# Attention in a hybrid diffusion step: a sixth PSUM bank, the waits of a pair of scores taken together, and the value products moved ahead of the next turns

## The chip, the cores and the metric

The kernel runs on one core of a Trainium2 chip. The metric is the device time in microseconds (us) of one execution. The kernel before takes 1153.21 us, the median of 3 runs (1152.54 to 1154.63).

The engines are named as in the profile: PE is TensorE (its matmuls; PEld is its weight loads), DVE is VectorE, ACT is ScalarE, POOL is GpSimd, SP is SyncE. Each engine works through its own program in order and stops at a wait until another engine has raised a semaphore. PSUM, where PE puts its results, has 8 banks of 512 float32 numbers for each of the 128 partitions.

## The reference: what is computed

Two trunk layers on 384 tokens (128 context tokens and 256 latent tokens) of width 1024, in float32. The even layer runs a Mamba-2 scan and latent attention (MLA, 8 heads) side by side, the odd layer grouped-query attention (GQA, 16 query heads of width 64); each ends with a mixture of 16 experts. What the change touches is the attention of both layers:

```
def block_attention(q, k, v):            # queries in blocks of 128
    ...
        s = jnp.einsum('bqgrd,bkgd->bgrqk', qi, k, preferred_element_type=jnp.float32) * scale
        p = jax.nn.softmax(s, axis=-1).astype(v.dtype)
        return jnp.einsum('bgrqk,bkgv->bqgrv', p, v)
```

The context tokens see 128 keys. The latent tokens see 384 keys: 128 of a cache and their own 256. With three blocks of 128 queries a head has three such tiles, so there are 24 tiles in MLA and 48 in GQA.

## The kernel before, in words

The program is written by hand, engine by engine, and the order in the text is the order in which an engine works. In the attention, the unit u is one tile of 128 queries of one head. `unit(u)` (L226) gives the head and the block: heads go in pairs, and the six units of a pair are block 0 of both heads (128 keys), block 1 of both, block 2 of both (384 keys each).

A unit goes through these steps:

- PE, L482: the scores, 128 queries by 128 or 384 keys, into a PSUM bank. In MLA the operands have 96 rows, in GQA 64; the two heads of a GQA pair stand in different halves of the 128 rows.
- DVE, L1293: minus the maximum of each row.
- ACT, L910: the exponential, from the bank into one of four buffers in `Pb` (unit u uses buffer u modulo 4), and the row sums. Ahead of it ACT waits for three things: the scores, the maximum, and the turn of unit u-4, which must have left the same buffer: `if u >= 4: after((kind, "pT", u - 4))`, in `exponential`.
- DVE, L1298 and L1300: one over the row sum, and the scaling.
- PE, L489: the turn, that is one or three 128x128 transposes, into another bank.
- ACT, L925: the turned rows are copied out of the bank into a turned-row buffer. There are two buffers, one for each head of a pair, so the copy of block 0 of a later pair first waits until the value products of the pair before are done (`pv_done`).
- PE, L504 and L507, in `values`: when all six units of a pair are turned and copied (`pt_ready`), the products of the values and the turned rows, for both heads, into bank 5 or 6.
- DVE, L1310, in `pair_out`: the result out of the bank.

PE and ACT go through the units in steps of two. In the step that begins at unit `first`, PE puts the scores of units first and first+1, then the turns of units first-4 and first-3 (`AHEAD` is 4), and then, in every third step, the value products of the pair whose last turns were in the step before. ACT puts the exponentials of units first and first+1, then the copies of units first-4 and first-3. So in the step with the value products of one pair, the scores and exponentials are those of block 2 of the next pair, and the turns and copies those of block 0 of that next pair.

The banks: every result that PE leaves in PSUM for ACT or DVE is a "job", listed once for the whole program (`job`, `attention_jobs`), with the engine that empties it. Job j goes into bank j modulo 5 (`RB` is 5), and `fill` makes PE wait until job j-5 has been emptied. The value products have banks 5 and 6 for themselves, bank 7 holds the rows of the modulation (`modulation`, L1219 to L1228, reads them; the call with part 2 stands behind the MLA attention in DVE's program).

Of the kernel before, what the change touches and what calls it, by code (L numbers as in the profile page):

```python
# [26 lines left out]
NT = T // P  # L27
# [47 lines left out]
def build(nc, small_d, x_d, w_d, y_d, stf_d, stb_d, ckv_d, kpe_d, gk_d, gv_d):  # L75
# [7 lines left out]
    with ctx:  # L83
# [67 lines left out]

        m_att = region(3072 + CONV_C * 385 + 3072 + 1536, 4 * 384, 2 * 896, 24, 24)
        lsq, lr_both = hTt[:, 0:1152], hTt[:, 1152:1920]
        lr = [lr_both[:, 0:384], lr_both[:, 384:768]]
# [6 lines left out]
        gss = [gss[:, HQ * t:HQ * (t + 1)] for t in range(NT)] + [gss[:, NT * HQ + HKV * t:NT * HQ + HKV * (t + 1)] for t in range(NT)]  # L161
        g_att = [gP, gPT, gnm, grs]
        qkv3 = qkv.rearrange("p (t n) -> p t n", t=NT)
        gkT3 = gkT.rearrange("p (h n) -> p h n", h=HKV)
        gqT3 = hTt[:, :].rearrange("p (h n) -> p h n", h=8)
# [47 lines left out]
        jobs = []  # L213
# [95 lines left out]
        free_of = {"A": S["free_act"], "D": S["free_dve"]}  # L309
        bank = lambda j: ps[:, j % RB, :]  # L310

# [79 lines left out]
        def _(pe):  # L391
            at = [0]

            def fill(*name):

                j = at[0]
                assert jobs[j][0] == name, (jobs[j], name)
                if j >= RB:
                    by, n = emptied[j - RB]
                    pe.wait_ge(free_of[by], n)  # L400
                at[0] += 1
                return bank(j)
# [68 lines left out]
            def attention(kind, heads, q_of, k_of, v_of, places):  # L471

                Pb, PTb = places[:2]
                base = 0 if kind == "mla" else NT * HM
                pairs = 0 if kind == "mla" else HM // 2
                for first in range(0, NT * heads + AHEAD, 2):
                    for u in (first, first + 1):
                        if u < NT * heads:
                            h, t = unit(u)
                            k0, nk = KEYS[t]  # L480
                            b = fill(kind, "s", u)
                            filled(mm(b[:, 0:nk], q_of(t, h), k_of(h, k0, nk), start=True, stop=True))  # L482
                    for v in (first - AHEAD, first - AHEAD + 1):
                        if v >= 0:
                            h, t = unit(v)
                            pe.wait_ge(S["p_ready"], base + v + 1)
                            b = fill(kind, "pT", v)
                            for k in range(KEYS[t][1] // P):
                                ins = pe.transpose(b[:, P * k:P * k + P], Pb[:, 384 * (v % 4) + P * k:384 * (v % 4) + P * k + P], ident)  # L489
                            filled(ins)  # L490
                    done = first - AHEAD
                    if done > 0 and done % 6 == 0:
                        values(done // 6 - 1, base, pairs, v_of, PTb)
                values(heads // 2 - 1, base, pairs, v_of, PTb)

            def values(k, base, pairs, v_of, PTb):
                pe.wait_ge(S["pt_ready"], base + 2 * NT * (k + 1))
# [3 lines left out]
                rows = [slice(0, 64), slice(64, 128)]  # L501
                pt = [PTb[:, 896 * i:896 * i + 896] for i in range(2)]
                for i in range(2):
# [272 lines left out]
            for k in range(N_PREP + 1):  # L776
# [11 lines left out]
                if k:  # L788
                    pe.wait_ge(S["qk_ready"], k)
                    for hh in range(2):  # L790
# [3 lines left out]
                        filled(ins)  # L794
            pe.wait_ge(S["qkT_ready"], 2 * N_PREP)
            attention("mla", HM, lambda t, h: mqT3[0:QM, h, TILE[t]], lambda h, k0, nk: mkT3[0:QM, h, k0:k0 + nk],
                      lambda s, h: mv3[:, s, 64 * h:64 * h + 64], m_att)
# [43 lines left out]
        def _(act):  # L841
# [56 lines left out]
            def attention(kind, heads, places):  # L898
                Pb, PTb, nm, rs = places
                base = 0 if kind == "mla" else NT * HM  # L900
# [14 lines left out]
                def turned(v):  # L915
                    h, t = unit(v)
                    b = take(kind, "pT", v)
                    if t == 0 and h >= 2:
                        act.wait_ge(S["pv_done"], base // NT + h // 2 * 2)
                    pt = PTb[:, 896 * (h % 2):896 * (h % 2) + 896]  # L920
                    out, src = pt[:, 0:P], b[:, 0:P]
# [264 lines left out]
        def _(dve):  # L1186
# [96 lines left out]
            def attention(kind, heads, places, out):  # L1283
                Pb, PTb, nm, rs = places
                base = 0 if kind == "mla" else NT * HM
# [303 lines left out]
            for k in range(N_PREP + 1):  # L1589
# [10 lines left out]
                if k:  # L1600
                    v = k - 1
                    s = v - NT
                    t = v if s < 0 else s
                    on = t in (1, 2)
                    qk_norm(v, cut(mkt[v % 2], HM), HM, QM, sm("q_norm" if s < 0 else "k_norm"), mss[v % 2], cut(msq[v % 2], HM),
                            rot("cos_e", t, ROPE) if on else None, rot("sin_e", t, ROPE) if on else None, NOPE)
                    dve.sem_inc(S["qk_ready"], 1)
            attention("mla", HM, m_att, oTm3)
            modulation(2)
            residual(0, 2, "out")  # L1610
# [204 lines left out]
```

## Time and profile before

| | |
|---|---|
| median of 3 runs | 1153.21 us (1152.54 to 1154.63) |
| the profiled execution's own time | 1165.88 us |
| its span in the trace | 1163.0 us |
| mean granted clock of TensorE | 0.892 of full speed |
| MLA attention, first scores to the output projection | 403.2 to 440.8 us of the span |
| GQA attention, first scores to the output projection | 821.2 to 897.2 us of the span |
| PE, DVE, ACT busy over the span | 80%, 32%, 26% |

The profiled execution is one run, 12.67 us above the median of the runs without a profile. All durations and positions below are of that execution. A view of the order of work gives for each group of instructions its start and duration and, in brackets, how long its engine stood idle before it and what the idle time ended with. "ACTq" as a releaser is ACT's sequencer, which raises a semaphore by an instruction of its own, as in the hand-back of a PSUM bank at L913 and L927. "issue" is a wait for nothing that the profile shows. "PEclk" is the mean granted clock of TensorE in the stretch, as a share of full speed (2.4 GHz); its lower level is 0.5 (1.2 GHz).

### The profile page before, as it was taken

To read this page: it belongs to the slowest core of one execution; us is meant where nothing else is said; L and a number is where in the kernel's file an instruction comes from. 1 tells how busy PE (TensorE), PEld (TensorE's weight loads), DVE (VectorE), ACT (ScalarE), POOL (GpSimd) and SP (SyncE) were. 2 spreads that over 40 slices of the span, in tenths; PEclk is the share of its full clock that TensorE was granted. 3 is DMA by queue.
4 is the path that set the end of the run, shared out by engine and by line. 5 is a ranking of instruction groups with operands and counts; after the bars stand their busy time and mean duration, and the time that the engine had idled before them with its cause. 6 is when DMAs were issued, how large, how long until landed. Compare 5 with 4: busy or idle time off the path is not lost.

```text
span 1163.0 us, 13763 instructions
## 1 busy us (share of the span) xinstructions
PE 934.8 (80%) x5481; PEld 488.7 (42%) x5481; DVE 375.5 (32%) x918; ACT 297.4 (26%) x690; POOL 50.3 (4%) x63
## 2 busy tenths in 40 slices
PE   5999985777886689972999991799898972999992
PEld 1455643555643445532323321455444532323321
DVE  0322015655734470042111101444664142101113
ACT  1421031232424370040201111311665140101111
POOL 0300000000000000102000001000000102000001
PEclk8899998978978799985999995799789985999995
DMA  9999994542464401215599997004100125599934
GB/s 387 427 424 413 413 420 203 214 163 109 158 239 162 168 1 55 109 55 198 226 408 424 424 425 283 0 1 179 47 1 1 58 105 205 234 412 414 418 144 181
DMA packets 36193, 258.96 MB, mean 223 GB/s; under 512 B 3392, under 2 KB 3536, under 8 KB 21152
## 3 DMA queue, kind: packets, MB, share of 16 engines
q1 hardware_dynamic: 20304, 198.27, 42.5%
q0 software_dynamic: 12224, 47.01, 10.2%
q10 hardware_dynamic: 3600, 12.78, 2.7%
q8 instruction: 45, 0.74, 0.3%
q14 instruction: 20, 0.16, 0.0%
HBM read 203.17 MB, written 54.87 MB: 222 GB/s over the span
## 4 chain that ended last, share of the span: by engine, by line
PE 66%; DVE 14%; DMA 8%; ACT 6%; issue 3%; POOL 1%; another core or an unknown queue 1%; POOLq 0%; SPq 0%; DVEq 0%; ACTq 0%
PE ps L468 20%; PE ps L580 12%; PE ps L602 7%; PE ps L817 6%; DMA U<-expert_rows 3%; DMA expert_rows<-U 3%; PE ps L482 3%; PE ps L564 2%; PE ps L432 2%; DMA ring<-w_in 2%; PE ps L507 2%; PE ps L736 2%; PE ps L489 1%; PE ps L528 1%; DVE U L1535 1%
## 5 line engine op out<-in xcount | busy, mean ns | idle before, releaser
L580 PE MATMUL ps<-ring,U 128*32 128x512 f32 x1200 | 166.3, 592 | 0.0
L468 PE MATMUL ps<-U,ring 128*128 128x384 f32 x320 | 105.1, 487 | 2.7 <-DVE U L1310 1.4
L602 PE MATMUL ps<-ring,U 128*32 128x512 f32 x672 | 85.7, 594 | 0.0
L580 PEld LDWEIGHTS ps<-ring,U 128*32 128x32 f32 x1200 | 47.5, 110 | 85.4 <-issue 85.4
L468 PEld LDWEIGHTS ps<-U,ring 128*128 128x128 f32 x320 | 60.0, 189 | 47.4 <-issue 4.2
L580 PE MATMUL ps<-hT,U 128*32 128x512 f32 x168 | 73.1, 592 | 0.0
L580 PE MATMUL ps<-U 128*32 128x512 f32 x168 | 73.1, 592 | 0.0
L817 PE MATMUL ps<-ring,hT 128*128 128x384 f32 x192 | 65.9, 503 | 5.8 <-ACT hT L895 4.9
L432 PE MATMUL ps<-ring,cond_w 128*32 128x384 f32 x512 | 58.3, 581 | 14.5 <-ACT cond_w L872 8.6
L468 PE MATMUL ps<-hT,ring 128*128 128x384 f32 x208 | 68.6, 488 | 1.0 <-issue 1.0
L564 PE MATMUL ps<-small,U 128*128 128x128 f32 x192 | 31.8, 318 | 44.7 <-DMA U<-expert_rows 42.5
L1393 DVE TENSOR_TENSOR U<-ps,U 128x256 f32<-128x256 f32 x24 | 10.1, 422 | 135.0 <-ACT U L963 135.0
L468 PEld LDWEIGHTS ps<-hT,ring 128*128 128x128 f32 x208 | 39.0, 190 | 30.0 <-issue 4.0
L817 PEld LDWEIGHTS ps<-ring,hT 128*128 128x128 f32 x192 | 37.3, 197 | 33.3 <-issue 9.6
L482 PE MATMUL ps<-U,hT 64*128 64x128 f32 (+3 forms) x144 | 48.6, 513 | 3.2 <-ACTq L913 1.6
L564 PEld LDWEIGHTS ps<-small,U 128*128 128x128 f32 x192 | 24.6, 162 | 54.5 <-DMA U<-expert_rows 48.5
L1401 DVE COPY U<-ps 128x512 f32<-128x512 f32 x24 | 16.6, 692 | 93.9 <-PE ps L602 53.6
L651 PE MATMUL ps<-small,U 128*128 128x128 f32 x48 | 11.8, 426 | 43.4 <-DVE U L1431 43.4
L884 ACT ACTIVATE hT<-xT 128x384 f32<-128x384 f32 x32 | 15.2, 516 | 110.1 <-DVE xT L1252 105.6
L963 ACT ACTIVATE U<-ps 128x256 f32<-128x256 f32 x24 | 9.3, 386 | 131.7 <-PE ps L580 131.7
L1252 DVE SCALAR_TENSOR_TENSOR xT<-ps,misc,xT 128x128 f32<-128x128 f32 (+1 forms) x32 | 11.9, 412 | 96.0 <-PE ps L468 96.0
L468 PE MATMUL ps<-ring,hT 128*128 128x384 f32 (+1 forms) x144 | 42.0, 451 | 0.5 <-issue 0.5
(251 smaller groups left out, 1337.8 us busy)
## 6 DMA issues: line engine op xcount, KB each, us to landing
ring<-w_in SPq DMA_DIRECT2D x102, 1536.0 KB, 11.2
expert_rows<-U POOLq DMA_DIRECT2D x16, 2048.0 KB, 73.1
U<-expert_rows SPq DMA_DIRECT2D x24, 512.0 KB, 6.0
expert_rows<-U ACTq DMA_DIRECT2D x24, 512.0 KB, 9.5
hT<-w_in SPq DMA_DIRECT2D x6, 1536.0 KB, 12.6
U<-w_in SPq DMA_DIRECT2D x6, 1536.0 KB, 15.8
small<-small_in SPq DMA_DIRECT2D x1, 3147.5 KB, 34.3
xT<-x_in SPq DMA_DIRECT2D x1, 1536.0 KB, 16.7
```

The source lines that it names most:

```text
L432: ins = mm(ps[q:q + 32, bank_row, 0:384], cond3[:, k, :], w[:, k, :], start=(k < 4), stop=(k >= 4))
L468: ins = mm(out, lhs(k), rhs(k), start=(k == 0), stop=(k == n - 1))
L482: filled(mm(b[:, 0:nk], q_of(t, h), k_of(h, k0, nk), start=True, stop=True))
L507: ins = mm(ps[rows[i], 5 + pair % 2, P:T], v_of(1 + c, 2 * k + i), pt[i][:, P + 256 * c:P + 256 * c + 256], start=(c == 0), stop=(c == NT ...
L564: ins = pe.transpose(ps[:, 3 + h, P * c:P * c + P], xgb[i % NR][:, 512 * h + P * c:512 * h + P * c + P], ident)
L580: ins = mm(ps[q:q + 32, r, :], xgT[:, r, P * k + q:P * k + q + 32], w[e][:, c:c + 512], start=(k == 0), stop=(k == DC - 1))
L602: ins = mm(ps[q:q + 32, 6 + h, :], actT_of[i % NR][:, P * j + q:P * j + q + 32], w[e][:, c:c + 512], start=(j == 0), stop=(j == 1))
L736: ins = mm(ps[:, 5 + q // 2, 64 * hh:64 * hh + 64], dec[u % 3][:, P * h:P * h + P], xdt[d][:, 64 * (4 * q + h):64 * (4 * q + h) + 64], sta ...
L817: ins = mm(b[:, 0:384], hT[:, k, TILE[t]], w[:, k, :], start=(k == 0), stop=(k == DC - 1))
L884: A(hT[:, c, :], xT[:, c, :], ACT.Square).then_inc(S["sq_ready"], 1)
L1252: ins = stt(xT[:, c, SEG[s]], b[:, SEG[s]], gt[:, 2 * c + s:2 * c + s + 1], xT[:, c, SEG[s]], MUL, ADD)
L1401: dve.tensor_copy(ysb[i % 2][:, 512:1024], ps[:, 7, :]).then_inc(S["y_dve"], 1)
```

## The change

In the attention of both layers:

- Bank 7 joins the five banks of the jobs while attention jobs are filled. Which bank a job gets is now worked out in a list, the bank longest unused first, and `fill` waits for the job that last had that bank. With six banks the pattern of four jobs to a step (two scores, two turns) gives the scores the banks of the turns two steps back, and the turns the banks of the scores one step back.
- PE waits for the banks of both scores of a pair before it puts the first, so the two score products stand next to each other without a wait between them.
- The value products of a step stand behind its scores and ahead of its turns; before, they stood behind its turns.
- GQA has four buffers of turned rows instead of two (two of them in the rows of queries that are no longer needed), and the copy of block 0 waits for the value products of two pairs back. MLA keeps its two buffers.
- Bank 7 must be free for the MLA attention: DVE's `modulation(2)`, which reads it, stands ahead of the attention, and PE waits for it (`mod_ready`).

The exponential's wait for the turn of unit u-4, the number of `Pb` buffers, and all instructions with their shapes stay as they are.

```diff
+        m_att[1] = [m_att[1][:, 896 * i:896 * i + 896] for i in range(2)]
...
-        g_att = [gP, gPT, gnm, grs]
+        g_att = [gP, [gPT[:, 0:896], gPT[:, 896:1792], qkv3[:, 1, 0:896], qkv3[:, 2, 0:896]], gnm, grs]
...
-        bank = lambda j: ps[:, j % RB, :]
+        order, last, BANK, BEFORE = deque(range(RB)), {}, [], []
+        for j, (n, _) in enumerate(jobs):
+            if n[0] in ("mla", "gqa"):
+                if RB + 2 not in order:
+                    order.appendleft(RB + 2)
+            elif RB + 2 in order:
+                order.remove(RB + 2)
+            b = order.popleft()
+            order.append(b)
+            BANK.append(b)
+            BEFORE.append(last.get(b))
+            last[b] = j
+        bank = lambda j: ps[:, BANK[j], :]
...
-                if j >= RB:
-                    by, n = emptied[j - RB]
+                if BEFORE[j] is not None:
+                    by, n = emptied[BEFORE[j]]
                     pe.wait_ge(free_of[by], n)
...
                 for first in range(0, NT * heads + AHEAD, 2):
-                    for u in (first, first + 1):
-                        if u < NT * heads:
+                    if first < NT * heads:
+                        b2 = [fill(kind, "s", u) for u in (first, first + 1)]
+                        for u in (first, first + 1):
                             h, t = unit(u)
                             k0, nk = KEYS[t]
-                            b = fill(kind, "s", u)
-                            filled(mm(b[:, 0:nk], q_of(t, h), k_of(h, k0, nk), start=True, stop=True))
+                            filled(mm(b2[u - first][:, 0:nk], q_of(t, h), k_of(h, k0, nk), start=True, stop=True))
+                    done = first - AHEAD
+                    if done > 0 and done % 6 == 0:
+                        values(done // 6 - 1, base, pairs, v_of, PT)
                     for v in (first - AHEAD, first - AHEAD + 1):
...
-                    done = first - AHEAD
-                    if done > 0 and done % 6 == 0:
-                        values(done // 6 - 1, base, pairs, v_of, PTb)
...
-                    if t == 0 and h >= 2:
-                        act.wait_ge(S["pv_done"], base // NT + h // 2 * 2)
-                    pt = PTb[:, 896 * (h % 2):896 * (h % 2) + 896]
+                    if t == 0 and h >= len(PT):
+                        act.wait_ge(S["pv_done"], base // NT + h // 2 * 2 - len(PT) + 2)
+                    pt = PT[h % len(PT)]
...
             pe.wait_ge(S["qkT_ready"], 2 * N_PREP)
+            pe.wait_ge(S["mod_ready"], len(PARTS))
             attention("mla", HM, lambda t, h: mqT3[0:QM, h, TILE[t]], lambda h, k0, nk: mkT3[0:QM, h, k0:k0 + nk],
...
+            modulation(2)
             attention("mla", HM, m_att, oTm3)
-            modulation(2)
```

PE's program in the GQA attention, in the step that holds the value products of the first pair, with the semaphores that each row waits for; `ps` is PSUM, `U` the work area, `hT` holds the queries and `small` the identity. The rows of before are the scores of block 2 (L482), the turns of block 0 (L489), the value products (L504, L507) and the scores of the next step:

```order
L482 MATMUL ps<-U,hT 128x384 [waits free_act] x2
L489 MATMUL ps<-small,U 128x128 [waits free_act,p_ready] x2
L504 MATMUL ps<-U 64x128 [waits pt_ready]
L504 MATMUL ps<-U 64x128
L507 MATMUL ps<-U,small 64x256 x2
L507 MATMUL ps<-U 64x256 x4
L482 MATMUL ps<-U,hT 128x128 [waits free_act] x2
```

The same place in the changed program, where L495 are the scores, L505 the turns, L517 and L520 the value products:

```order
L495 MATMUL ps<-U,hT 128x384 [waits free_act]
L495 MATMUL ps<-U,hT 128x384
L517 MATMUL ps<-U 64x128 [waits pt_ready]
L517 MATMUL ps<-U 64x128
L520 MATMUL ps<-U,small 64x256 x2
L520 MATMUL ps<-U 64x256 x4
L505 MATMUL ps<-small,U 128x128 [waits free_act,p_ready] x2
L495 MATMUL ps<-U,hT 128x128 [waits free_act]
L495 MATMUL ps<-U,hT 128x128
```

The two turns have moved behind the value products, with their wait for `pt_ready` ahead of them, and the second score of each pair has lost its wait for a bank.

DVE's program at the beginning of the MLA attention, before (L1279 ends the preparation of the keys, L1293 are the first maxima):

```order
L1278 TENSOR_TENSOR U<-U 128x768
L1279 TENSOR_TENSOR U<-U,small 128x768
L1293 TENSOR_REDUCE U<-ps 128x1 x2
L1298 RECIPROCAL U<-U 128x1
L1300 TENSOR_SCALAR U<-U 128x128
```

and now, where L1240 is the modulation's one instruction:

```order
L1292 TENSOR_TENSOR U<-U 128x768
L1293 TENSOR_TENSOR U<-U,small 128x768
L1240 TENSOR_TENSOR misc<-ps,small 128x96
L1307 TENSOR_REDUCE U<-ps 128x1 x2
L1312 RECIPROCAL U<-U 128x1
```

The modulation stands ahead of the first maxima; before, it stood behind the last copy of the attention.

## Rows read from the trace of the kernel before

**Rows 1.** The page's busy times over the span, three engines of its section 1.
```profile
PE 934.8 (80%) x5481; PEld 488.7 (42%) x5481; DVE 375.5 (32%) x918; ACT 297.4 (26%) x690; POOL 50.3 (4%) x63
```

**Rows 2.** Busy time by stretch: two GQA turns and one of MLA.
```profile
core 0: us, PE busy (x) PEld busy (x) DVE busy (x) ACT busy (x) POOL busy (x), PEclk, DMA share, GB/s
863.74:871.91 8.17, 7.64 (x43) 4.00 (x43) 5.86 (x19) 6.06 (x18) 0.00 (x0) 1.00 0.01 2
...
425.07:433.26 8.19, 7.58 (x42) 4.21 (x42) 5.77 (x19) 6.06 (x18) 0.00 (x0) 1.00 0.00 1
```

**Rows 3.** Order of work on ACT, one GQA turn at full clock.
```profile
866.56 0.37 ACT L910 ACTIVATE U<-ps,U 128x128 f32<-128x128 f32 x1 [0.21 <-PE ps L489]
...
867.81 1.08 ACT L925 COPY U<-ps 128x384 f32<-128x384 f32 x2
869.10 0.58 ACT L910 ACTIVATE U<-ps,U 128x384 f32<-128x384 f32 x1 [0.21 <-PE ps L489]
...
870.77 1.08 ACT L925 COPY U<-ps 128x384 f32<-128x384 f32 x2
872.07 0.58 ACT L910 ACTIVATE U<-ps,U 128x384 f32<-128x384 f32 x1 [0.21 <-DVE U L1293]
872.95 0.58 ACT L910 ACTIVATE U<-ps,U 128x384 f32<-128x384 f32 x1 [0.21 <-ACT U L910]
873.80 0.27 ACT L925 COPY U<-ps 128x128 f32<-128x128 f32 x1 [0.18 <-PE ps L507]
```

**Rows 4.** Order of work on PE and DVE in the same turn.
```profile
870.84 0.30 PE L489 MATMUL ps<-small,U 128*128 128x128 f32 x1
...
871.44 0.30 PE L489 MATMUL ps<-small,U 128*128 128x128 f32 x1 [0.30 <-DVE U L1300]
...
871.91 0.44 PE L504 MATMUL ps<-U 128*64 128x128 f32 x4 [0.17 <-ACT U L925]
...
872.61 1.03 PE L507 MATMUL ps<-U 128*64 128x256 f32 x8
...
873.57 0.49 PE L482 MATMUL ps<-U,hT 64*128 64x128 f32 x4
873.72 0.56 DVE L1310 COPY U<-ps 128x384 f32<-128x384 f32 x1 [0.33 <-PE ps L507]
```

**Rows 5.** Waits in the GQA attention, then in the MLA attention.
```profile
PEld ps L482 <- ACTq L913: 6.5, 13, 0.9
...
PEld ps L482 <- ACTq L927: 1.4, 6, 0.2
...
PEld ps L482 <- ACTq L913: 4.0, 8, 0.7
...
PEld ps L482 <- ACTq L927: 0.7, 3, 0.2
```

**Rows 6.** Order of work on PE, then on ACT: value products at the lower clock.
```profile
844.06 0.69 PE L504 MATMUL ps<-U 128*64 128x128 f32 x4 [0.16 <-ACT U L925]
...
847.24 0.51 PE L482 MATMUL ps<-U,hT 64*128 64x128 f32 x4
```
```profile
847.45 0.27 ACT L925 COPY U<-ps 128x128 f32<-128x128 f32 x1 [1.68 <-PE ps L507]
...
857.29 0.27 ACT L925 COPY U<-ps 128x128 f32<-128x128 f32 x1 [1.57 <-PE ps L507]
...
891.63 0.27 ACT L925 COPY U<-ps 128x128 f32<-128x128 f32 x1 [1.67 <-PE ps L507]
```

**Rows 7.** Busy time and granted clock by stretch, MLA and GQA.
```profile
407.00:440.80 33.80, 28.23 (x161) 15.68 (x159) 21.74 (x71) 23.33 (x68) 0.00 (x0) 1.00 0.01 1
821.20:833.70 12.50, 11.66 (x35) 6.48 (x36) 7.48 (x26) 7.92 (x23) 0.00 (x0) 0.50 0.03 10
...
843.90:847.30 3.40, 3.24 (x18) 1.72 (x18) 0.71 (x3) 1.45 (x5) 0.00 (x0) 0.50 0.02 5
```

**Rows 8.** Order of work on ACT at the beginning of the GQA attention.
```profile
829.92 0.37 ACT L910 ACTIVATE U<-ps,U 128x128 f32<-128x128 f32 x1 [0.41 <-PE ps L489]
...
833.08 0.58 ACT L910 ACTIVATE U<-ps,U 128x384 f32<-128x384 f32 x1 [0.82 <-PE ps L489]
```

**Rows 9.** Order of work on DVE around the MLA attention.
```profile
403.80 0.56 DVE L1293 TENSOR_REDUCE U<-ps 128x1 f32<-128x128 f32 x2 [5.01 <-PE ps L482]
...
440.63 0.25 DVE L1226 TENSOR_TENSOR misc<-ps,small 128x96 f32<-128x96 f32 x1
```

More of the change, by code:

```diff
@@ L471, in attention @@
             def attention(kind, heads, q_of, k_of, v_of, places):
-                Pb, PTb = places[:2]
+                Pb, PT = places[:2]
                 base = 0 if kind == "mla" else NT * HM
@@ L490, in attention, with values @@
                             filled(ins)
-                    done = first - AHEAD
-                    if done > 0 and done % 6 == 0:
-                        values(done // 6 - 1, base, pairs, v_of, PTb)
-                values(heads // 2 - 1, base, pairs, v_of, PTb)
-            def values(k, base, pairs, v_of, PTb):
+                values(heads // 2 - 1, base, pairs, v_of, PT)
+            def values(k, base, pairs, v_of, PT):
                 pe.wait_ge(S["pt_ready"], base + 2 * NT * (k + 1))
@@ L501, in values @@
                 rows = [slice(0, 64), slice(64, 128)]
-                pt = [PTb[:, 896 * i:896 * i + 896] for i in range(2)]
+                pt = [PT[(2 * k + i) % len(PT)] for i in range(2)]
                 for i in range(2):
@@ L898, in attention @@
             def attention(kind, heads, places):
-                Pb, PTb, nm, rs = places
+                Pb, PT, nm, rs = places
                 base = 0 if kind == "mla" else NT * HM
@@ L1283, in attention @@
             def attention(kind, heads, places, out):
-                Pb, PTb, nm, rs = places
+                Pb, _, nm, rs = places
                 base = 0 if kind == "mla" else NT * HM
```

## The prediction

> **What bounds the kernel now.** I read the page first, then the order of work inside the two attentions, since the change touches nothing else. Over the span PE is busiest and ACT is at 26% [rows 1], which says nothing about this stage. A stretch from one start of the value products to the next is the time of one pair of heads (a turn of the loop, three steps): 8.17 us in GQA, 8.19 in MLA, at full clock in both [rows 2]. The two agree, though the scores of MLA have 96 rows and cannot stand beside each other in the array as those of GQA might; PE is busy 7.6 of the 8.2 us and ACT 6.06, so by busy time PE looks like the bound [rows 2].
>
 The reader is to see in rows 3 that the exponential at 872.07 starts 0.22 us behind the copies that end at 871.85 (870.77 + 1.08), and in rows 4 that PE begins the value products at 871.91, released by the same copies. The two run beside each other. They can, because the two turns of block 0, which this exponential and its neighbour wait for, stand on PE ahead of the values, at 870.84 and 871.44 [rows 4].
>
> PE's waits are real as waits: its score loads waited 6.5 + 1.4 us in GQA and 4.0 + 0.7 in MLA for ACT to hand back a bank [rows 5]. But they end when ACT, the slower of the two, gets there.
>
> **The change, part by part.** Sums are made against the profiled execution (span 1163.0 us, own time 1165.88); the median of the runs is 12.67 us less. I carry the difference over to the median unscaled.
>
> Values ahead of turns. In the step with value products, ACT's exponential of unit u (block 2) waits for the turn of unit u-4, which is the turn of block 0 of the next pair. In the changed order this turn stands behind the value products on PE. The value products in turn wait for `pt_ready`, that is for the two copies which ACT makes directly ahead of that exponential. So ACT, which had the values beside its exponentials, now has them in its chain: copies, values, turn, exponential. Step by step, from 871.85, where the copies end:
> - to the start of the values 0.06 us (871.91) [rows 4];
> - the values until PE takes its next instruction, 873.57 - 871.91 = 1.66 us [rows 4];
> - one transpose, 0.30 us [rows 4];
> - from PE's end to the next engine, 0.08 us (the last value product ends at 872.61 + 1.03 = 873.64, DVE's copy starts at 873.72) [rows 4].
>
> That puts the exponential at 873.95 instead of 872.07, 1.88 us later. The second exponential needs the second transpose, which is ready long before its turn 0.88 us later. Queued behind ACT's waiting exponential are the second exponential and the copies of block 0; everything on ACT moves by 1.88 us, and nothing gives it back, as ACT has no idle time in the rest of the turn. The next turn takes about 8.17 + 1.88 = 10.05 us. Value products stand inside the loop 3 times in MLA (4 pairs, the last behind the loop) and 7 times in GQA (8 pairs): 10 x 1.88 = +18.8 us. The shortest the rows allow is the 1.66 and the 0.06 alone, less the 0.21 that ACT needs anyhow: 1.51 us, 15.1 in all. The longest is values to their last end (1.73), 0.06, 0.30, and a hand-over to ACT of 0.21 as before its exponentials: 2.30 - 0.21 = 2.09, 20.9 in all. I take 1.88, which is the sum of the neighbours' own rows.
>
> At the lower clock the values take 847.24 - 844.06 = 3.18 us instead of 1.66, and before, ACT already stood idle 1.68, 1.57 and 1.67 us for them at three of the seven GQA pairs [rows 6]. There the new chain is longer by 1.52 and the old wait of about 1.5 (less the 0.18) goes away, so these three add the same 1.9 us each.
>
> Sixth bank and the joint wait. They take away PE's waits for ACT's hand-backs [rows 5] and let the two GQA scores of a pair run side by side. At full clock this is beside ACT's chain and worth nothing. Its cover is gone where PE is the slower one: the beginning of GQA, at half clock up to 833.7 us [rows 7], where ACT waited 0.41 and 0.82 us for PE, 0.81 us more than its 0.21 each time [rows 8]. I take -0.8 us; the bounds are 0 and, for all four bank waits of rows 5, -12.6, which is a rival below. The joint wait itself can hold a first score back for the second's bank; both are banks of turns two steps back, which ACT emptied a step before, so I put it at nothing.
>
> Four turned-row buffers. They free the copy of block 0 from the pair before; but that copy now stands behind a turn that stands behind the same values. At full clock it waited for nothing (0.18 us is the fixed cost). Nothing.
>
> Modulation and its wait. It takes 0.25 us behind the attention [rows 9]. DVE is idle 5.01 us ahead of the first maximum of MLA [rows 9], which hides it, and PE's wait for it stands where PE waits for ACT's last copies anyhow. Without this cover it would cost 0.25 us.
>
> The clock. PE gets longer pauses for the same work: a turn of 10.05 us holds what 8.17 held. In GQA PE fell to the lower clock for three short stretches inside the loop, each time at value products [rows 6, 7]; in MLA from 407 us on it never did [rows 7]. Each new such stretch that holds value products costs 3.18 - 1.66 = 1.52 us on the chain. I take one to two more, +2.3 us; the bounds are 0 and 7 x 1.52 = 10.6.
>
> Sum: 18.8 - 0.8 + 2.3 = +20.3 us, so 1153.2 + 20.3 = 1173.5 us. In the profiled execution I expect MLA some 6 us longer and GQA some 14.
>
> **Rivals.**
>
> Banks were the bound (faster). PE waits at L482 for ACT's hand-back in nearly every step, and by busy time PE is the fullest engine. If PE's waits set the pace, taking them away gives back up to 6.5 + 1.4 + 4.0 + 0.7 = 12.6 us [rows 5]: 1140.6 us. It decides if ACT has slack of more than 1.9 us in a turn, so that the late exponential is absorbed. For it: PE's 7.6 us of 8.17 [rows 2]. Against it: the constant gaps of ACT [rows 3], and that MLA and GQA turns last the same. The Trainium skill, on its page "Perfetto Trace Analysis", section "Optimization Strategy", says that the same gap repeating on the engine that should be saturated can mean too few buffers in SBUF or PSUM. By that rule the sum would be this rival's 1140.6. The trace shows the repeating gap on PE, but not that PE is the engine to be saturated here.
>
> The values are early enough (no change). If the value products could start before ACT's copies end, only the transpose behind them would be late, 873.57 + 0.30 + 0.08 = 873.95 against the copy at 873.80: 0.15 us for each of the ten, 1154.7 us. It would need the exponential not to wait for that turn, or `pt_ready` to be asked for an earlier unit. The program has both waits unchanged, and rows 4 show the values starting 0.06 us behind the copies. Only a slip in my reading speaks for it.
>
> The clock falls with the pauses (slower still). If PE loses full clock at all seven of the ten value products that had it, the sum is 18.8 - 0.8 + 10.6 = +28.6 us, 1181.8 us. For it: three falls in GQA already, with pauses of 0.3 us. Against it: MLA has none in 33.8 us [rows 7], and the value products themselves are dense work. The Trainium skill describes it on the page "TensorE: Matmul & The Clock Gate", section "A second HAM failure mode: psum-queue depth-cycling": short idle times of PE between groups, as PSUM banks are cycled, make the clock swing between its two levels. By that the sum would be this rival's 1181.8; the trace agrees for GQA in three places and disagrees for MLA.
>
> **How the numbers follow.** My forecast has 0.80, the clock rival 0.14, no change 0.03, the banks 0.03. What can be told from no change is about 0.2%, 2.3 us. The forecast's own bounds are 15.1 - 0.8 = +14.3 and 20.9 - 0.8 + 4.6 (three slow stretches) = +24.7, so 1167.5 to 1177.9. To hold the time 8 times in 10 I let the range reach to the clock rival: 1167 to 1182. Slower by over 0.2%: 0.94; within: 0.03; faster: 0.03.
>
> **What would show it.** Right: in a turn, ACT has one idle time of about 2 us, ahead of the block 2 exponential, put down to PE's turn, and it follows the copies and covers the value products; the other gaps stay at 0.21 and 0.12 to 0.18. A turn lasts about 10 us. The waits of the scores for ACT's bank hand-back shrink and the GQA scores of a pair overlap, with no gain. DVE is idle 2 to 3 us once in a turn. Nothing outside the two attentions changes length. Wrong: turns of 8.2 us or less with a 0.21 gap there, or turns of 10 us in one attention only, or a change of time in the scan or the experts.

## The result, and the profile after

The changed kernel takes 1177.11 us, the median of 4 runs (1171.84 to 1187.82). The kernel before, run on the same chip beside it, takes 1153.15 us (1152.54 to 1154.63, 4 runs). The ratio is 1.0192, with a 95% interval of 1.0137 to 1.0247: slower by 1.4 to 2.5%. The forecast was 1173.5 us, in a range of 1167 to 1182. Here and below, ratios and intervals are computed from the single runs, without those in a slower state, so they are not exactly the quotients of the medians.

The profiled execution took 1187.82 us, with a span of 1185.9 us, the longest of the four. It stands 10.71 us above its median, much as that of before does (12.67). Its stages, and the same of the profile before, in us:

| stage | before | after | difference |
|---|---|---|---|
| start to the first MLA scores | 403.17 | 406.07 | +2.90 |
| MLA attention | 37.60 | 45.28 | +7.68 |
| output projection | 64.10 | 66.65 | +2.55 |
| experts, and the projections of the odd layer | 316.29 | 315.28 | -1.01 |
| GQA attention | 76.06 | 85.87 | +9.81 |
| output projection | 42.80 | 45.27 | +2.47 |
| last experts | 222.95 | 221.44 | -1.51 |

The attentions and the projections behind them are 22.5 us longer together, of the 22.9 us between the two spans. The ratio gives 0.0192 x 1153.15 = 22.1 us, so these four stages hold the loss.

Busy time and granted clock by stretch, of the kernel after (columns as in [rows 2]). The first row is a turn of the loop in MLA, the second one in GQA. The other three are the beginning of MLA, and the last value products of each attention with the start of the output projection:

```profile
430.40:440.44 10.04, 7.31 (x42) 4.38 (x42) 5.70 (x20) 6.07 (x18) 0.00 (x0) 1.00 0.00 1
857.13:867.16 10.03, 6.31 (x43) 3.39 (x43) 5.71 (x20) 6.05 (x18) 0.00 (x0) 1.00 0.00 1
...
406.10:412.20 6.10, 6.10 (x13) 3.58 (x14) 3.45 (x13) 3.54 (x9) 0.00 (x0) 0.50 0.10 40
446.30:456.50 10.20, 8.40 (x24) 4.53 (x25) 0.56 (x1) 0.95 (x2) 0.00 (x0) 0.50 0.00 0
917.40:924.20 6.80, 6.12 (x14) 3.10 (x11) 0.56 (x1) 0.00 (x0) 0.00 (x0) 0.50 0.00 0
```

A turn has gone from 8.17 and 8.19 us [rows 2] to 10.03 and 10.04. All engines do the work they did: ACT 6.05 us against 6.06, DVE 5.71 against 5.86. PE in GQA is even less busy, 6.31 us against 7.64. A longer turn with no more work is a longer chain. The order of work on ACT shows where it is:

```profile
856.01 1.07 ACT L939 COPY U<-ps 128x384 f32<-128x384 f32 x2
859.25 0.58 ACT L924 ACTIVATE U<-ps,U 128x384 f32<-128x384 f32 x1 [2.17 <-PE ps L505]
...
860.12 0.58 ACT L924 ACTIVATE U<-ps,U 128x384 f32<-128x384 f32 x1 [0.20 <-ACT U L924]
...
860.97 0.27 ACT L939 COPY U<-ps 128x128 f32<-128x128 f32 x1 [0.17 <-ACT U L924]
...
862.53 0.37 ACT L924 ACTIVATE U<-ps,U 128x128 f32<-128x128 f32 x1 [0.20 <-ACT U L924]
```

One gap of 2.17 us stands where [rows 3] have 0.21, and it is put down to a turn, L505. The others are what they were. The order of work on PE in the same turn shows what this turn stands behind:

```profile
857.13 0.44 PE L517 MATMUL ps<-U 128*64 128x128 f32 x4 [1.88 <-ACT U L939]
857.40 0.60 PE L520 MATMUL ps<-U,small 128*64 128x256 f32 x4
...
857.84 1.03 PE L520 MATMUL ps<-U 128*64 128x256 f32 x8
...
858.80 0.44 PE L505 MATMUL ps<-small,U 128*128 128x128 f32 x2
859.17 0.49 PE L495 MATMUL ps<-U,hT 64*128 64x128 f32 x4
...
864.36 0.92 PE L495 MATMUL ps<-U,hT 64*128 64x384 f32 x4 [0.67 <-ACTq L941]
```

ACT's copies end at 857.08 (856.01 + 1.07). The values start at 857.13, the turn behind them at 858.80, ACT's exponential at 859.25. Each step of the chain is there. PE now stands idle 1.88 us ahead of the values (in [rows 4]: 0.17), and ACT 2.17 us behind them: the two engines wait for each other in turn. The last row is a pair of GQA scores without a wait between them: their four records span 0.92 us, and PE is idle 0.67 us ahead of them for a bank.

DVE (the first row is the modulation, in its new place):

```profile
403.31 0.26 DVE L1240 TENSOR_TENSOR misc<-ps,small 128x96 f32<-128x96 f32 x1 [2.79 <-PEq L451]
...
407.02 0.61 DVE L1307 TENSOR_REDUCE U<-ps 128x1 f32<-128x128 f32 x2 [3.44 <-PE ps L495]
```

The waits of the kernel after, in GQA and then in MLA (columns as in [rows 5]: us in total, times, longest):

```profile
PEld ps L517 <- ACT U L939: 18.5, 8, 2.5
ACT U L924 <- PE ps L505: 18.3, 12, 3.8
...
PEld ps L495 <- ACTq L941: 7.8, 12, 0.9
...
ACT U L924 <- PE ps L505: 7.4, 4, 2.2
...
PEld ps L495 <- ACTq L941: 3.2, 6, 0.6
```

A sixth bank did not remove PE's waits for banks in GQA: the score loads waited 7.8 us for L941 and once 1.2 us for L927, against 6.5 + 1.4 in [rows 5]. The waits have changed hands: L941 hands back a bank of copied turns, where L913 handed back a bank of scores. The turns now wait for L927, the hand-back of the scores: 4.5 us, against 0.6 us for turns before. So the change moved the waits of PE and did not take them away.

### The profile page after: what moved, and what is told of

Its sections match the earlier page's. It is cut to its first block, busy times and chain, and to the rows that moved or that the text cites. A ratio compares the mean times of both kernels' runs of the same rounds, so it can differ in the third digit from the quotient of the medians.

```text
span 1185.9 us, 13795 instructions
## 1 busy us (share of the span) xinstructions
PE 935.6 (79%) x5481; PEld 490.7 (41%) x5481; DVE 375.2 (32%) x918; ACT 297.6 (25%) x690; POOL 50.4 (4%) x63
## 4 chain that ended last, share of the span: by engine, by line
PE 64%; DVE 13%; DMA 8%; ACT 8%; issue 4%; POOL 1%; another core or an unknown queue 1%; ACTq 0%; POOLq 0%; SPq 0%; DVEq 0%
PE ps L481 19%; PE ps L593 12%; PE ps L615 7%; PE ps L831 6%; DMA U<-expert_rows 3%; DMA expert_rows<-U 3%; PE ps L577 2%; ACT U L924 2%; ACT U L939 2%; PE ps L495 2%; PE ps L445 2%; DMA ring<-w_in 2%; PE ps L749 2%; PE ps L520 2%; DVE U L1549 1%
## 5 line engine op out<-in xcount | busy, mean ns | idle before, releaser
L481 PE MATMUL ps<-U,ring 128*128 128x384 f32 x320 | 110.1, 505 | 2.7 <-DVE U L1324 1.4
L481 PEld LDWEIGHTS ps<-U,ring 128*128 128x128 f32 x320 | 62.5, 197 | 50.7 <-issue 8.9
L495 PE MATMUL ps<-U,hT 64*128 64x128 f32 (+3 forms) x144 | 39.3, 532 | 9.2 <-ACTq L941 6.9
L924 ACT ACTIVATE U<-ps,U 128x384 f32<-128x384 f32 (+1 forms) x72 | 36.8, 510 | 37.2 <-PE ps L505 25.7
L664 PE MATMUL ps<-small,U 128*128 128x128 f32 x48 | 11.8, 427 | 42.8 <-DVE U L1445 42.8
```

What stands on the lines that cost most here:

```text
L481: ins = mm(out, lhs(k), rhs(k), start=(k == 0), stop=(k == n - 1))
L495: filled(mm(b2[u - first][:, 0:nk], q_of(t, h), k_of(h, k0, nk), start=True, stop=True))
L924: A(Pb[:, 384 * (u % 4):384 * (u % 4) + nk], b[:, 0:nk], ACT.Exp, bias=nm[:, u:u + 1], accum_out=rs[:, u:u + 1]).then_inc(S["e_ready"], 1)
```

## The experiments

Two theories were put to the test. By the first, the new time is a chain: the value products stand between ACT's copies and the turn that ACT's next exponential waits for. By the rival, it comes from the banks: the joint wait, or the sixth bank's new pattern.

**Value products back behind the turns.** All else of the change stays.

```diff
-                    done = first - AHEAD
-                    if done > 0 and done % 6 == 0:
-                        values(done // 6 - 1, base, pairs, v_of, PT)
                     for v in (first - AHEAD, first - AHEAD + 1):
...
                             filled(ins)
+                    done = first - AHEAD
+                    if done > 0 and done % 6 == 0:
+                        values(done // 6 - 1, base, pairs, v_of, PT)
```

> The changed kernel with the value products put back behind the turns of the step; sixth bank, joint wait, four turned-row buffers and the moved modulation stay. Theory (the turn of block 0 behind the values puts the values into ACT's chain): turns of 8.2 us again, ACT's gap ahead of the block 2 exponential 0.21 us, time 1152 to 1154 us. Rival (the new bank order, the joint wait and a lower clock that follows from them are the cost): turns stay near 9 to 10 us or PE falls to the lower clock more often, time 1162 us or more. Second rival (PE's bank waits were the bound and are now gone): turns below 8 us, time 1141 to 1147 us.

Measured: 1157.75 us (1153.67 to 1166.92, 12 runs) beside 1153.66 of before (23 runs), ratio 1.0028, interval 0.9995 to 1.0061. The loss is gone, though the time is above the 1152 to 1154 us that I had expected. There is no gain either: the sixth bank, the joint wait and the four buffers together are worth nothing that can be measured. They were not put in one by one, but for the joint wait (below). The order of work on ACT, of this kernel, has the old short gaps behind the copies and ahead of block 0:

```profile
838.79 1.07 ACT L939 COPY U<-ps 128x384 f32<-128x384 f32 x2
840.06 0.58 ACT L924 ACTIVATE U<-ps,U 128x384 f32<-128x384 f32 x1 [0.20 <-DVE U L1307]
...
841.78 0.27 ACT L939 COPY U<-ps 128x128 f32<-128x128 f32 x1 [0.17 <-PE ps L520]
```

The turn that holds it, by stretch, shows PE busy for 1.5 us less than in [rows 2] and the turn only 0.1 us shorter:

```profile
838.79:846.83 8.04, 6.09 (x42) 3.48 (x42) 5.83 (x20) 6.06 (x18) 0.00 (x0) 1.00 0.01 3
```

**Only the value products moved.** The kernel before, with five banks and single waits, and the same three lines of `values` ahead of the turns.

```diff
+                    done = first - AHEAD
+                    if done > 0 and done % 6 == 0:
+                        values(done // 6 - 1, base, pairs, v_of, PTb)
                     for v in (first - AHEAD, first - AHEAD + 1):
...
-                    done = first - AHEAD
-                    if done > 0 and done % 6 == 0:
-                        values(done // 6 - 1, base, pairs, v_of, PTb)
```

> The kernel before with one edit, the value products ahead of the turns of the step; five banks, single waits, two turned-row buffers. Theory: the whole loss, turns of about 10.1 us in both attentions, one idle time of about 2.0 to 2.2 us on ACT ahead of the block 2 exponential, time 1170 to 1178 us. Rival (the loss needs the sixth bank and the joint wait): turns of at most 9 us, time below 1162 us.

Measured: 1181.15 us (1176.46 to 1182.57, 4 runs), ratio 1.0228, interval 1.0175 to 1.0282. One edit brings the whole loss; its interval overlaps that of the full change. The turns are 10.13 us at full clock, as expected, and the time is above the expected 1170 to 1178 us. On ACT the same gap:

```profile
426.52 1.08 ACT L925 COPY U<-ps 128x384 f32<-128x384 f32 x2
...
429.78 0.58 ACT L910 ACTIVATE U<-ps,U 128x384 f32<-128x384 f32 x1 [2.18 <-PE ps L492]
```

Its GQA attention is 92.44 us in the profile, 6.6 more than that of the full change, because the clock was low for longer there, as one stretch shows:

```profile
884.10:901.00 16.90, 16.32 (x55) 8.98 (x54) 8.21 (x26) 9.06 (x27) 0.00 (x0) 0.50 0.00 0
```

**Six exponential buffers.** The changed kernel, but the exponential of unit u waits for the turn of unit u-6, which is ahead of the values again. This leaves the values where the change put them and cuts the chain.

```diff
+        g_att = [[gP[:, 384 * i:384 * i + 384] for i in range(4)] + [gPT[:, 384 * i:384 * i + 384] for i in range(2)],
+                 [gPT[:, 896:1792]] + [qkv3[:, i, 0:896] for i in range(3)], gnm, grs]
...
-                    if u >= 4:
-                        after((kind, "pT", u - 4))
+                    if u >= 6:
+                        after((kind, "pT", u - 6))
```

> The changed kernel, values ahead of the turns as in it, with six buffers for the exponentials instead of four, so that the exponential of unit u waits for the turn of unit u-6 and not u-4. Theory: the exponentials of block 2 run beside the value products again and only the copy of block 0 is late, by about 0.15 us: turns of 8.3 to 8.4 us, time 1153 to 1157 us. Rival (what costs is the place of the values among PE's work, whatever the exponential waits for): turns stay at 10.0 us, time 1170 us or more.

Measured: 1160.61 us (1156.57 to 1169.62, 10 runs), ratio 1.0077, interval 1.0036 to 1.0118. Turns at full clock take 8.31 us in MLA and 8.33 to 8.34 in GQA, as expected; the time is above the expected 1153 to 1157 us. The order of work on ACT, then on PE:

```profile
829.90 0.65 ACT L941 COPY U<-ps 128x128 f32<-128x128 f32 x2 [0.33 <-PE ps L507]
...
835.07 1.08 ACT L941 COPY U<-ps 128x384 f32<-128x384 f32 x2
836.36 0.58 ACT L926 ACTIVATE U<-ps,U 128x384 f32<-128x384 f32 x1 [0.21 <-DVE U L1309]
```

```profile
836.21 0.44 PE L519 MATMUL ps<-U 128*64 128x128 f32 x4 [1.91 <-ACT U L941]
```

The exponential at 836.36 now runs beside the values, which begin at 836.21.

The gap of 2.17 us is gone with the values still ahead of the turns, so it is the wait for u-4 that makes them cost, and not their place as such. What stays is the turn itself: the copies of block 0 wait for it 0.33 us instead of 0.17. Ten times 0.14 us are 1.4 us of the 4 to 14 us that the interval gives; the rest is not shown. In its profile the two attentions are 3.0 us longer than before (38.30 and 78.36 us), and PE fell to the lower clock at five value products in GQA, against three before.

**Block 0 copied by DVE.** ACT's chain is 6.05 us of busy time and its fixed gaps. Here the value products are behind the turns and the copies of block 0 go from ACT to DVE, behind the scaling of the pair's last unit.

```diff
-                    job((kind, "pT", u - AHEAD), "A")
+                    job((kind, "pT", u - AHEAD), "A" if unit(u - AHEAD)[1] else "D")
...
+                    if v >= 0 and v % 6 == 5:
+                        for x in (v - 5, v - 4):
+                            h = unit(x)[0]
+                            b = take(kind, "pT", x)
...
+                            dve.tensor_copy(PT[h % len(PT)][:, 0:P], b[:, 0:P]).then_inc(S["pt0_ready"], 1)
```

> As e1 (values behind the turns, six banks, joint wait, four turned-row buffers), and the copies of the turned rows of block 0, two in a turn of the loop, made by DVE instead of ACT. Theory (ACT's own chain is the pace of both kernels): ACT's chain is shorter by two copies with their gaps, 2 x 0.45 us, turns of about 7.3 us in both attentions, time 1142 to 1147 us. Rival (PE is the pace at 8.2 us): turns stay at 8.1 to 8.2 us, time 1152 to 1154 us. Second rival (DVE's new wait for the turn holds up the maxima): turns of 8.5 us or more.

Measured: 1167.57 us (1161.02 to 1176.56, 6 runs), ratio 1.0132, interval 1.0075 to 1.0189. The expected gain is a loss, as the second rival had it: turns at full clock take 9.12 to 9.14 us, the first one of GQA 8.93. A stretch of MLA at full clock, on DVE and then on ACT:

```profile
421.58 0.56 DVE L1335 COPY U<-ps 128x384 f32<-128x384 f32 x1 [0.33 <-PE ps L521]
422.05 0.28 DVE L1309 TENSOR_REDUCE U<-ps 128x1 f32<-128x128 f32 x1
...
422.77 0.28 DVE L1327 COPY U<-ps 128x128 f32<-128x128 f32 x1
423.28 0.29 DVE L1327 COPY U<-ps 128x128 f32<-128x128 f32 x1 [0.22 <-DVE U L1327]
423.72 0.29 DVE L1309 TENSOR_REDUCE U<-ps 128x1 f32<-128x128 f32 x1
```

```profile
422.60 0.37 ACT L925 ACTIVATE U<-ps,U 128x128 f32<-128x128 f32 x1 [1.13 <-PE ps L502]
...
424.10 0.37 ACT L925 ACTIVATE U<-ps,U 128x128 f32<-128x128 f32 x1 [1.04 <-DVE U L1309]
```

DVE's order is: the result of the value products (L1335), the first maximum of block 0 (L1309), the copies of block 0 (L1327), the second maximum. ACT's two exponentials of block 0 wait 1.13 and 1.04 us. The second waits for its maximum, which DVE's copies have made late. For the first, the row names a turn, L502: the maximum was done at 422.33 (422.05 + 0.28), and the turn of unit u-4, which this exponential waits for too, came 0.15 us later by the trace's semaphores (422.49 against 422.34). So there are two more chains through the values, which I had left out of the forecast, and they end almost together. One is on PE alone: values, scores of block 0, turn of unit u-4, exponential of block 0. The other goes through DVE: values, copy of their result, maximum, exponential of block 0. ACT's own copies used to fill this time; without them it is idle.

**Everything one step later.** Six exponential buffers, four turned-row buffers in both attentions, block 0 copied by DVE, and the value products a step later, so that none of these chains should bind.

```diff
-                    done = first - AHEAD
+                    done = first - AHEAD - 2
...
-                    w = v - 10
+                    w = v - 12
```

> Sixth bank and joint wait; six exponential buffers and four turned-row buffers in both attentions; block 0 copies on DVE behind the scaling of block 2; the value products one step later (behind the scores of block 0 of the pair after next, ahead of its turns) and DVE's copy of their result two units later. Theory (e4 failed because the values, their copy by DVE and the next maximum form a second chain from ACT's last copy to the exponential of block 0, about as long as ACT's own): with the values out of that chain ACT's chain of 7.2 to 7.5 us is the pace, the attentions take 37 us (MLA) and 70 us (GQA), time 5 to 8 us below the kernel before. Rival (PE is the pace at 8.1 us whatever ACT does): turns of 8.1 us, time within 2 us of the kernel before.

Measured: 1153.45 us (1147.39 to 1164.29, 12 runs) beside 1155.43 of before (23 runs), ratio 0.9991, interval 0.9958 to 1.0025: no measurable gain. MLA takes 37.64 us and GQA 72.65, against 37.60 and 76.06 in the profile before. A turn came to 7.70 and 8.07 us in MLA and 8.06 to 8.21 in GQA at full clock, and not to the 7.2 to 7.5 us that I had expected. On ACT and DVE:

```profile
864.45 0.48 DVE L1329 COPY U<-ps 128x128 f32<-128x128 f32 x2
...
865.17 0.29 DVE L1311 TENSOR_REDUCE U<-ps 128x1 f32<-128x128 f32 x1 [0.24 <-PE ps L507]
```

```profile
865.55 0.37 ACT L927 ACTIVATE U<-ps,U 128x128 f32<-128x128 f32 x1 [1.00 <-DVE U L1311]
```

ACT saved the copies and waits 1.00 us for a maximum, which DVE makes late, behind the copies that it took over. The work left ACT, and the turn stayed, but for the one of 7.70 us.

**Value products twice, ahead of the turns.** The changed kernel with each value product done twice, to measure the chain by its slope. The output is the same.

```diff
-                for i in range(2):
-                    mm(ps[rows[i], 5 + pair % 2, 0:P], v_of(0, 2 * k + i), pt[i][:, 0:P], start=True, stop=True)
-                for c in range(NT):
+                for again in range(2):
...
-                        if c == NT - 1:
+                            if c == NT - 1 and again:
```

> The changed kernel with every value product computed twice into the same bank, the second time over the first; the result is the same. Theory (the values stand wholly in ACT's chain): each turn of 10.03 us grows by the 1.66 us of one more set, to 11.7 us at full clock, and ACT's one idle time from 2.2 to about 3.8 us. Rival (part of the 2 us idle time is something else than the values): turns of 11 us or less.

Measured: 1202.65 us (one run). Turns at full clock take 11.65 and 11.67 us in MLA, 11.52 and 11.64 in GQA, and the gap on ACT is 3.68 us:

```profile
864.59 1.08 ACT L940 COPY U<-ps 128x384 f32<-128x384 f32 x2
...
869.36 0.58 ACT L925 ACTIVATE U<-ps,U 128x384 f32<-128x384 f32 x1 [3.68 <-PE ps L505]
```

The turn is 1.62 us longer (11.65 - 10.03) and the gap 1.51 us (3.68 - 2.17), about the 1.66 us that the values take [rows 4]. The values are in ACT's chain with about their full length.

**Value products twice, behind the turns.** The same doubling in the kernel of the first experiment.

> As e1 (values behind the turns), with every value product computed twice. Theory of a second chain: from ACT's last copy through values, DVE's copy of the result and the maximum to the exponential of block 0 there are only about 0.3 us to spare, so turns grow by 1.66 less about 0.3, to 9.4 to 9.6 us. Rival (values there are beside ACT's work with room to spare, as PE idles for bank waits): turns of 8.1 to 8.6 us.

Measured: 1173.47 us (one run). Turns at full clock take 9.71 us in MLA and 9.62 in GQA, against 8.12 and 8.04 to 8.06 without the doubling, and a little above the expected 9.4 to 9.6. On ACT, on DVE and on PE:

```profile
846.43 0.58 ACT L925 ACTIVATE U<-ps,U 128x384 f32<-128x384 f32 x1 [0.21 <-ACT U L925]
...
849.66 0.37 ACT L925 ACTIVATE U<-ps,U 128x128 f32<-128x128 f32 x1 [1.67 <-PE ps L502]
```

```profile
848.71 0.56 DVE L1325 COPY U<-ps 128x384 f32<-128x384 f32 x1 [1.84 <-PE ps L521]
849.18 0.28 DVE L1308 TENSOR_REDUCE U<-ps 128x1 f32<-128x128 f32 x1
```

```profile
848.57 0.49 PE L495 MATMUL ps<-U,hT 64*128 64x128 f32 x4
848.99 0.88 PE L502 MATMUL ps<-small,U 128*128 128x128 f32 x6
```

The exponential of block 2 does not wait (0.21 us): the first chain is cut. But 1.57 to 1.59 of the 1.66 us come back at the exponential of block 0, by both of the other chains. On DVE the result is copied at 848.71 and the maximum made from 849.18 to 849.46. On PE the scores of block 0 start at 848.57 and the turns of block 1 at 848.99; the first of these is the turn of u-4 that the exponential waits for, and the row of ACT names it (L502). By the trace's semaphores it came at 849.55, the maximum at 849.48, so PE's chain ended last here, 0.07 us behind DVE's. With the values behind the turns there is next to no room either, 0.1 us or less by this difference (1.66 - 1.57). Which of the two chains would bind without the other was not tested.

**Without the joint wait.** The kernel of the first experiment, each score waiting for its own bank.

```diff
-                        b2 = [fill(kind, "s", u) for u in (first, first + 1)]
...
-                            filled(mm(b2[u - first][:, 0:nk], q_of(t, h), k_of(h, k0, nk), start=True, stop=True))
+                            b = fill(kind, "s", u)
+                            filled(mm(b[:, 0:nk], q_of(t, h), k_of(h, k0, nk), start=True, stop=True))
```

> As e1 (sixth bank, values behind the turns, four turned-row buffers), with the wait for the bank of the second score back between the two scores. Theory: nothing on ACT's chain, turns of 8.0 to 8.2 us at full clock, time within 2 us of e1; with six banks the second bank is free by then, so the GQA scores of a pair overlap as well. Rival (the joint wait is what lets the scores overlap and shortens the stretches at the lower clock): GQA 2 us longer or more than in e1.

Measured: 1157.92 us (1152.85 to 1170.72, 10 runs), ratio 1.0033, interval 0.9997 to 1.0069, the same as with the joint wait. One of its GQA turns at full clock, by stretch:

```profile
840.40:848.51 8.11, 6.70 (x42) 3.74 (x42) 5.86 (x21) 6.05 (x19) 0.00 (x0) 1.00 0.00 1
```

The joint wait brings PE's busy time from 6.70 to 6.09 us and the turn from 8.11 to 8.04, too little to show in the time. The rival's sign did appear in the profile: GQA takes 77.32 us, 2.06 more than in the first experiment (75.26), with five falls of the clock at value products against four. It is one profile of each, this one of the longest of its ten runs (1170.72 us), and the ratios are the same, so an effect of the joint wait on the clock is not shown.

## Why the prediction was right, point by point

- **The bound.** That ACT has no time to give back held: doubling the values ahead of the turns lengthened a turn by about their own time, and bringing PE's busy time down to 6.09 us in a turn left it at 8.04. PE's 7.6 busy us were not the bound. That ACT's own chain alone sets the pace, as the forecast has it, is not shown: with the values behind the turns, two chains through the values end within 0.1 us of ACT's own (the doubled values), and taking two copies off ACT made a turn longer. The constant gaps show that ACT never waits long, not that nothing else is as late. The forecast's 1.88 us did not need this, as ahead of the turns the values' chain is by far the latest.
- **Values ahead of turns, 10 x 1.88 = 18.8 us.** Measured 1.84, 1.85 and 1.90 in MLA (10.03 and 10.04 against 8.19, and 6.98 against 5.08 for the shorter last one), 1.86 in the mean, and 1.86 in a GQA turn at full clock (10.03 - 8.17). Ten times 1.86 is 18.6 us. The turn of 10.05 us is 10.03.
- **Sixth bank and joint wait, -0.8 us.** From the first scores to the first values GQA took 14.73 us before and takes 13.96 now: -0.77. It is the sixth bank that gives this: with only the values moved this stretch takes 14.73 us, with six banks and no joint wait 13.99. Beside ACT's chain at full clock the edit is worth nothing measurable, as forecast. I had said that the waits of the scores for banks would shrink. In MLA they did (3.2 us against 4.7), in GQA not (7.8 + 1.2 against 7.9).
- **Four buffers, modulation, 0.** GQA with four buffers has the same turn as MLA with two (10.03 and 10.04 us). DVE is still idle 3.44 us behind the modulation, ahead of the first maximum.
- **The clock, +2.3 us.** In the two profiles what is left for it is +4.7, and in another place than forecast: this is the mis-sized term. In the GQA loop the lower clock hit value products three times before (turns of 9.94 and 9.74 us, and 1.5 us of the last); after, it hit one (a turn of 11.77): with small differences of other turns -2.9 us. One of these, a turn of 10.31 us, is at full clock throughout; ACT waited 0.48 us instead of 0.20 ahead of one exponential there. The beginning of MLA is 0.6 us longer, at the lower clock up to 412.2. From the first scores to the first values it takes 14.30 us, and 14.33 to 14.36 in the first experiment and with doubled values, at a mean clock of 0.79; it takes 13.71 to 13.74 us in the three kernels without the joint wait (0.88). So here the clock and the joint wait can't be told apart. The last value products of both attentions fell to the lower clock (+1.5 and +0.5). The remaining +5.0 us stand in the two output projections, which I had said would not change: they begin at the lower clock, in the stretches 446.30:456.50 and 917.40:924.20. The projections are as long in the kernel with only the values moved (66.58 and 45.40 us), and at 64.1 and 42.8 in every other kernel profiled here, also in the one with doubled values ahead of the turns. So it came in both kernels with the values moved and not doubled, and in no other; why the clock fell there is open.
- **MLA some 6 us longer, GQA some 14.** 7.7 and 9.8, for the same reason. 18.6 - 0.8 + 4.7 = 22.5 us is the difference of the four stages; the 4.7 is what the other two terms leave. That the sum came out so close is in part luck: the attentions grew by 17.5 us and not 20.3, and the 5.0 us of the projections, which the forecast had at nothing, made up for it. By the letter of the signs of being wrong, a change outside the attentions did come: 2.5 us in each projection. The stages ahead of MLA and of the experts changed by 2.9, -1.0 and -1.5 us.
- **The rivals.** The banks' 1140.6 us did not come: with six of them and the values put back, PE's busy time in a turn is 6.09 us instead of 7.64, and the turn 8.04 instead of 8.17. The waits for banks are still there in that kernel (7.7 + 1.2 us in GQA), so no run shows one without them. The rule of the Trainium skill (page "Perfetto Trace Analysis", section "Optimization Strategy"), that a repeating gap can mean too few buffers, did not help in the kernel before: the gaps on PE ended when ACT got there, and the sixth bank gave nothing. It fits the kernel after, where a gap of 2.17 us repeats on ACT, the engine to be saturated: two more exponential buffers in SBUF take most of it back. "No change" is refuted. The clock rival gave 1181.8 us by a fall at each of the value products; one of the seven value products in the GQA loop fell, so its mechanism did not come about, though more than the forecast's 2.3 us is left for the clock. At 1177.11 us the median lies 3.6 us above the forecast and 4.7 below this rival, so the time alone would not have told them apart.

## What to carry to other kernels

Where an engine shows the same small gap ahead of each instruction, whatever releases it, it has no time to give back, even at 26% busy over the whole kernel; here a bank for the engine that waits for it bought nothing. It need not be the only one that sets the pace: other chains can end just ahead of it and hide in its gaps. Before moving a block of work ahead of another on an in-order engine, list who waits for the block that becomes late: here an exponential four units on, through a buffer it reuses. And look for the other chains through the block: work taken off ACT came back as waits for a turn on PE and for a late maximum on DVE.

## What the runs showed of the hardware

- **A wait for a transfer goes with some 10 us more, in either kernel.** The stage ahead of MLA takes 392 to 408 us in ten profiles. In three of them DVE stood idle for a transfer, by the profile, in the scan; DVE's rows in the kernel before, in that without the joint wait (both with the wait), and in that with only the values moved (without it):

```profile
189.63 1.23 DVE L1571 TENSOR_TENSOR U<-hT,U 128x1024 f32<-128x1024 f32 x1 [8.56 <-DMA expert_rows<-U]
```

```profile
191.20 1.23 DVE L1585 TENSOR_TENSOR U<-hT,U 128x1024 f32<-128x1024 f32 x1 [12.77 <-DMA expert_rows<-U]
```

```profile
182.37 1.22 DVE L1571 TENSOR_TENSOR U<-hT,U 128x1024 f32<-128x1024 f32 x1
```

  The third profile with this wait is the one after (10.59 us). The stage takes 403 to 408 us in these three and 392 to 398 in the other seven, though no edit touches it. Single runs of one kernel lie up to 20 us apart (1147.77 to 1168.09 for 23 runs of before). This wait is about half of that, so the totals of one profile of each kernel can't be compared. That the transfer alone makes the stage longer is not shown.
- **Two scores of 64 rows take much less time than two of 96 once no wait stands between them.** The four records of a pair span 0.92 us in GQA (864.36), in the kernel before, with a wait between, 1.39 and 1.79 (866.63 and 868.99). In MLA, with 96 rows, the same four span 1.53 us; PE's row of the kernel after:

```profile
417.57 1.53 PE L495 MATMUL ps<-U,hT 96*128 96x384 f32 x4 [0.32 <-ACTq L941]
```

- **ACT's gap hardly depends on the releaser:** 0.20 or 0.21 us ahead of an exponential and 0.17 or 0.18 ahead of a copy of block 0, wherever the rows shown here have no wait for work.
